# A diffusion block's head: modulation made chunk by chunk beside the first products, and sums of squares on TensorE

## The chip, the cores and the metric

One core of one Trainium2 chip. The metric is the device time in microseconds of one execution; the median of three runs is given. The compute engines are TensorE (PE; its weight loads are PEld), VectorE (DVE), ScalarE (ACT) and GpSimd (POOL); SyncE (SP) issues nearly all loads.

## What is computed

Two transformer-like blocks one after the other on 512 latent tokens (and 256 context tokens in the first part) of 1024 features, in fp32. The change touches the first norm and what feeds the first product:

```
m_l = split(silu(c) @ ada_w + ada_b, 9)        # for the latent tokens; m_c alike with c_ctx
x   = x   + 0.5 * m_l[2] * swiglu(modulate(rms_norm(x,   norm1_w), m_l[0], m_l[1]), w1, w3, w2)
ctx = ctx + 0.5 * m_c[2] * swiglu(modulate(rms_norm(ctx, norm1_w), m_c[0], m_c[1]), w1, w3, w2)
rms_norm(x, w)       = x * rsqrt(mean(x * x) + eps) * w
modulate(h, shift, scale) = h * (1 + scale) + shift
```

## The kernel before

Activations lie with the feature on the partition: 1024 features are eight chunks (KC = 8) of 128, the 768 tokens (TOK) the columns. Every large product is made of three matmuls in fp32r, whi with h_hi, whi with h_lo and wlo with h_hi. Weights come as panels of 128 x 1024 into a ring of four (raw); ScalarE rounds them to whi (round_panel, L707), GpSimd makes wlo = raw - whi (low_part, L654).

The head is all that comes before the first product. SP issues, in this order (L563 to L580): x_lat (2 MB), x_ctx (1 MB), eight small loads (vec, cond_s, lsig, lr_raw, two gate_sb, ident, rope_decay), six of the eight blocks of the modulation weights (ada_f, 1 MB each; a block holds 128 input features, the contraction index, for all 2048 columns of shift and scale), two panels, the other two blocks, two panels, and cond_b. ScalarE waits for vec and for the six transfers of small_loaded, makes the start of the log-sigmoids, Silu of the condition (cond_w), and squares x chunk by chunk (square, L724). VectorE makes the log-sigmoids (24 operations, L1807 to L1819) and adds the squares up (add_squares, L1465). TensorE does the first half of the modulation matmuls (first_modulation, L2405: four column groups of the array, 512 columns each, accumulated over the blocks into PSUM bank 5), waits for the sums and multiplies them with a column of 1/1024 (norm, L2387), spreads the factors over the partitions (L2377), does the second half of the modulation and, when ScalarE has copied the row out (L796), transposes it (L2411). VectorE adds the bias and 1 (L2248, L1456), and then, for each chunk in turn, scales x (prod, L1538); ScalarE makes h_hi (L807) and h32 (L811); VectorE makes h_lo (L1552).

The first pair of panels (first_pair, L2330) follows chunk by chunk: 12 matmuls of 384 columns for each, as soon as h_lo of the chunk is there (h_ready). Behind it stand the third panel (rounded_first, L2424) and the rest of the first layer (L2316). On VectorE the norm is followed by first_layer: differences of token halves (token_differences, L1614 to L1617), the modulation products of later parts, one chunk of 128 outputs at a time over a ring of three loads (ada_chunk, L1440), and the gated products (L1628). The first down product (first_down, L2482) needs gates from the first eight such chunks before the PSUM banks of its first panels come free (L1605).

Of the kernel before, what the change touches and what calls it, by code (L numbers as in the profile page):

```python
# [18 lines left out]
P = 128  # L19
# [16 lines left out]
ADA_COLS = ADA_PE * P  # L36
ADA_TILES = ADA_COLS // 512
# [20 lines left out]
for _s in STAGES:  # L58
# [20 lines left out]
                  gla_gate_b_b=2, conv_b_2=4, conv_w_2=16, rg_a_b_2=8, rg_x_b_2=8, rg_lambda_2=8)  # L79
# [4 lines left out]
N_VEC = _n  # L84

# [42 lines left out]
def build(nc, x_t, ctx_t, cond, ada_t, vecs, panels, lr_w, gate_w, decays, rope_grid, u_tab, level_masks, diag2, ident_h,  # L128
          ada_p, cond_t, mem_t, positions, rope_pp_h, window_bias, rg_w, out):
# [4 lines left out]
    with ExitStack() as stack:  # L134
# [34 lines left out]
        ada_f = [at(f"ada_f{kc}", ADA_COLS, R_H + 8 * kc * KB if kc < 6 else R_G + (24 + 8 * (kc - 6)) * KB) for kc in range(KC)]  # L169
        ada_row = at("ada_row", 512, R_G + 6 * KB)  # L170
        ada_w = at("ada_w", ADA_RING * D, R_ADA)
        cond_b = at("cond_b", 2 * D, R_ADA + 12 * KB)
        cond_s = at("cond_s", 2 * KC, R_TMP + 10 * KB)
        cond_w = at("cond_w", 32 * KC, R_TMP + 10 * KB + 128)
        ada_prod = at("ada_prod", D, R_ADA + 20 * KB, bf16)
        vec = at("vec", N_VEC, R_VEC)
        mods = at("mods", 2 * NMOD * KC, R_VEC + 800)
        scales = at("scales", 5 * KC, R_VEC + 1408)
        gates = at("gates", 4 * KC, R_VEC + 1664)
        eps_zero = at("eps_zero", 2, R_VEC + 1792)  # L180
        eps_t, zero_t = eps_zero[:, 0:1], eps_zero[:, 1:2]
# [7 lines left out]
        ident = at("ident", P, R_VEC + 5440)  # L189
# [51 lines left out]
        lsig = at("lsig", 16, R_VEC + 1568)  # L241
        nlsig_both = at("nlsig_both", 8, R_VEC + 1632)
        nlsig, lsig_ctx = nlsig_both[:, 0:4], nlsig_both[:, 4:8]
        ls_tmp = at("ls_tmp", 4 * 16, R_TMP + 11 * KB + 512)
# [19 lines left out]
        rope_decay = at("rope_decay", 6, R_VEC + 1376)  # L264
# [33 lines left out]
        x_loaded, vec_loaded, cond_loaded, consts = sem("x_loaded"), sem("vec_loaded"), sem("cond_loaded"), sem("consts")  # L298
# [142 lines left out]
        squares = [prod[:, 0:TOK], act_a[:, TOK:2 * TOK]]  # L441

# [119 lines left out]
        def _(sp):  # L562
            sp.dma_start(x_lat[:, :], x_t).then_inc(x_loaded, 16)  # L563
            sp.dma_start(x_ctx[:, :], ctx_t).then_inc(x_loaded, 16)
            sp.dma_start(vec[:, :], vecs).then_inc(vec_loaded, 16)
            sp.dma_start(cond_s[:, :], cond_t).then_inc(condt_loaded, 16)
            sp.dma_start(lsig[:, 0:8], decays.partition_broadcast(P)).then_inc(small_loaded, 16)
            sp.dma_start(lr_raw[:, :], lr_w).then_inc(small_loaded, 16)
            for d in range(2):
                sp.dma_start(gate_sb[d][:, :], gate_w[:, d * 256:(d + 1) * 256]).then_inc(small_loaded, 16)  # L570
            sp.dma_start(ident[:, :], ident_h).then_inc(small_loaded, 16)
            sp.dma_start(rope_pp[:, :], rope_pp_h).then_inc(small_loaded, 16)
            for kc in range(KC):
                if kc == KC - 2:
                    for s in range(2):
                        sp.dma_start(raw[:, s * PANEL:(s + 1) * PANEL], panels[s]).then_inc(raw_ready[s], 16)
                sp.dma_start(ada_f[kc][:, :], ada_p[kc]).then_inc(ada_loaded[kc], 16)
# [23 lines left out]
            first_panel(L1_DOWN[0] + 3)  # L601
            late = []
# [89 lines left out]
        def _(act):  # L692
# [21 lines left out]
            def square(m, kc):  # L714

                if m.n == 0:
                    act.wait_ge(x_loaded, 32)
                else:
                    act.wait_ge(down_evac, x_final(m.n) + kc + 1)
                if kc >= 3:  # L720
                    act.wait_ge(sum_done, m.n * (KC - 1) + kc - 2)
                buf = act_a[:, 0:TOK] if kc == 0 else squares[kc % 2]
# [59 lines left out]
            def split_gates():  # L782
                act.wait_ge(small_loaded, 96)
# [4 lines left out]
            def norm(m):  # L788
                act.wait_ge(stats_ready, m.n + 1)
                means = apart_means() if m.apart else bank(4, m.T // P)  # L790
                act.activation(rms[:, 0:m.T // P], means, ACT.Sqrt, bias=eps_t).then_inc(root_ready, 1)
                if m.n == 0:
                    round_panel(0, 1)
                    round_panel(1, 1)
                    act.wait_ge(ada_rows_done, 1)
                    act.activation(ada_row[:, :], bank(5), ACT.Copy).then_inc(ada_copied, 1)  # L796
                if m.last:
                    return
                for kc in range(KC):
# [9 lines left out]
                    if m.n == 0:  # L809
                        for j, (_, n, c0, _) in enumerate(m.segs()):  # L810
                            ins = act.activation(h32[kc][:, c0:c0 + n], prod[:, b + c0:b + c0 + n], ACT.Identity, bias=m.B[j](kc))  # L811
                        ins.then_inc(h32_done, 1)
                    if m.n == 0 and kc in (3, 4):
                        round_panel(kc - 1, 1)
# [548 lines left out]
            def cross_queries():  # L1363
# [8 lines left out]
            act.wait_ge(small_loaded, 96)  # L1372
            link(act.activation(lsig[:, 8:16], vcol("rg_lambda_2", 0, 8), ACT.Copy))
            link(act.activation(ls_tmp[:, 0:16], lsig[:, :], ACT.Abs))
            act.activation(ls_tmp[:, 0:16], ls_tmp[:, 0:16], ACT.Exp, scale=-1.0).then_inc(ls_exp, 1)
            act.wait_ge(condt_loaded, 16)
# [51 lines left out]
        def _(dve):  # L1428
# [98 lines left out]
            def norm(m):  # L1527
                if m.n:
# [1713 lines left out]
```

## Time and profile before

| What | Value |
|---|---|
| Time, median of 3 runs | 2044.85 us (2044.04 to 2046.57) |
| Profiled execution | 2042.27 us, span 2040.4 us |
| Mean granted clock of TensorE | 0.977 |
| TensorE busy | 1949.3 us (96%) |
| VectorE busy | 1024.0 us (50%) |
| ScalarE busy | 834.4 us (41%) |
| GpSimd busy | 833.7 us (41%) |
| Chain that ended last | TensorE 62%, issue 18%, VectorE 9%, GpSimd 7%, ScalarE 3% |
| First product of the first panels | 45.16 us after the span's start |

A busy share is an average over the whole span. The chain that ended last follows, from the last instruction backwards, what released each step; idle time of an engine that is not on it costs nothing. The clock column of a stretch is the granted TensorE clock as a share of 2.4 GHz.

### The profile page before, as it was taken

The page shows a single profiled execution, that of the slowest core. Times are in us where ns is not written, and L with a number is a line of the kernel's source. Part 1 is how long each engine was busy: PE and PEld are TensorE (multiplying, and loading weights), DVE is VectorE, ACT ScalarE, POOL GpSimd, SP SyncE. Part 2 cuts the span into 40 slices and gives each one's busy share as a digit, 9 for nine tenths or more (in the row PEclk, how much of TensorE's full clock was granted, in tenths as well). Part 3 has the DMA queues.
Part 4 walks back from the last instruction along what each step waited for, and adds up shares of the span by engine and source line. Part 5 has one row for each costly group of instructions (what it writes and reads, how often), then busy time and mean ns, then how long its engine had stood idle before and what let it go on. Part 6 is the DMA issues. An engine that isn't in the chain of part 4 may idle for free.

```text
span 2040.4 us, 25938 instructions
## 1 busy us (share of the span) xinstructions
PE 1949.3 (96%) x9514; PEld 1643.4 (81%) x9514; DVE 1024.0 (50%) x1527; ACT 834.4 (41%) x1276; POOL 833.7 (41%) x414
## 2 busy tenths in 40 slices
PE   4999999999989999889999999999899989999998
PEld 2999999999978875557888888877667767888886
DVE  4879877657457215964213112577964462122124
ACT  4425242434355135562532323447565453232231
POOL 1337574656424221442453443534512324353532
PEclk8999999999989999789999999999999999999999
DMA  8133343433312110002232232232211112232321
GB/s 352 53 134 141 131 163 109 160 135 115 113 62 73 72 71 31 11 21 88 83 113 93 87 108 93 103 124 83 93 52 52 65 60 93 90 107 83 113 83 62
DMA packets 53487, 197.68 MB, mean 97 GB/s; under 512 B 6320, under 2 KB 7056, under 8 KB 51600
## 3 DMA queue, kind: packets, MB, share of 16 engines
q1 hardware_dynamic: 52240, 191.47, 26.1%
q10 hardware_dynamic: 1152, 4.92, 0.7%
q8 instruction: 63, 1.03, 0.2%
q14 instruction: 32, 0.26, 0.0%
HBM read 194.27 MB, written 2.10 MB: 96 GB/s over the span
## 4 chain that ended last, share of the span: by engine, by line
PE 62%; issue 18%; DVE 9%; POOL 7%; ACT 3%; DMA 1%; SPq 0%; POOLq 0%; DVEq 0%; ACTq 0%
PE ps L2316 26%; PE ps L2445 13%; PE ps L2482 8%; POOL wlo L654 6%; PE ps L2330 2%; PE ps L2303 1%; PE ps L2304 1%; PE ps L2305 1%; PE ps L2847 1%; PE ps L2671 1%; PE ps L2662 1%; PE ps L2865 1%; DVE ada_prod L1440 1%; DVE act_a L1465 1%; DVE rg_t L2216 1%
## 5 line engine op out<-in xcount | busy, mean ns | idle before, releaser
L654 POOL TENSOR_TENSOR wlo<-raw,whi 128x1024 fp32r<-128x1024 f32 x244 | 600.0, 2469 | 985.0 <-ACT whi L707 961.6
L707 ACT ACTIVATE whi<-raw 128x1024 fp32r<-128x1024 f32 x244 | 253.6, 1053 | 271.1 <-PE ps L2316 188.4
L2316 PE MATMUL ps<-h_hi,whi 128*128 128x512 f32 (+1 forms) x960 | 352.9, 382 | 2.9 <-DVE act_a L1597 1.7
L2316 PE MATMUL ps<-h_hi,wlo 128*128 128x512 f32 (+1 forms) x960 | 350.6, 380 | 0.0
L2316 PE MATMUL ps<-h_lo,whi 128*128 128x512 f32 (+1 forms) x960 | 350.0, 379 | 0.0
L661 POOL TENSOR_TENSOR wlo<-raw,whi 128x512 fp32r<-128x512 f32 x108 | 160.3, 1499 | 133.5 <-ACT whi L875 133.1
L2316 PEld LDWEIGHTS ps<-h_hi,whi 128*128 128x128 f32 x960 | 176.6, 188 | 40.6 <-issue 5.8
L2316 PEld LDWEIGHTS ps<-h_lo,whi 128*128 128x128 f32 x960 | 176.2, 188 | 33.5 <-issue 1.0
L2316 PEld LDWEIGHTS ps<-h_hi,wlo 128*128 128x128 f32 x960 | 176.3, 188 | 32.7
L2316 PE MATMUL ps<-g_hi,whi 128*128 128x512 f32 x432 | 168.0, 389 | 0.0
L2316 PE MATMUL ps<-g_lo,whi 128*128 128x512 f32 x432 | 168.0, 389 | 0.0
L2316 PE MATMUL ps<-g_hi,wlo 128*128 128x512 f32 x432 | 168.0, 389 | 0.0
L1440 DVE SCALAR_TENSOR_TENSOR ada_prod<-ada_w,cond_b 128x1024 bf16<-128x1024 f32 x80 | 130.2, 1628 | 1.6
L875 ACT ACTIVATE whi<-raw 128x512 fp32r<-128x512 f32 x108 | 66.7, 627 | 150.2 <-PE ps L2482 113.4
L1605 DVE SCALAR_TENSOR_TENSOR x_lat<-ps,gates,x_lat 128x384 f32<-128x384 f32 (+2 forms) x120 | 59.7, 530 | 115.3 <-PE ps L2316 72.2
L1595 DVE TENSOR_TENSOR prod<-act_a,ps 128x512 f32<-128x512 f32 x22 | 15.1, 688 | 170.3 <-PE ps L2316 165.0
L2445 PE MATMUL ps<-h_hi,whi 128*128 128x384 f32 x288 | 96.3, 334 | 0.0
L2445 PE MATMUL ps<-h_lo,whi 128*128 128x384 f32 x288 | 96.3, 334 | 0.0
L2445 PE MATMUL ps<-h_hi,wlo 128*128 128x384 f32 x288 | 96.2, 334 | 0.0
L2316 PEld LDWEIGHTS ps<-g_lo,whi 128*128 128x128 f32 x432 | 81.1, 188 | 16.9
L2316 PEld LDWEIGHTS ps<-g_hi,whi 128*128 128x128 f32 x432 | 81.1, 188 | 16.9
L2316 PEld LDWEIGHTS ps<-g_hi,wlo 128*128 128x128 f32 x432 | 81.1, 188 | 16.8
(483 smaller groups left out, 3744.3 us busy)
## 6 DMA issues: line engine op xcount, KB each, us to landing
raw<-panels SPq DMA_DIRECT2D x280, 512.0 KB, 3.2
ada_w<-ada_t SPq DMA_DIRECT2D x56, 512.0 KB, 3.7
ada_f<-ada_p SPq DMA_DIRECT2D x8, 1024.0 KB, 17.0
x_lat<-x_t SPq DMA_DIRECT2D x1, 2048.0 KB, 8.0
out<-x_lat SPq DMA_DIRECT2D x8, 256.0 KB, 2.2
x_ctx<-ctx_t SPq DMA_DIRECT2D x1, 1024.0 KB, 10.0
cond_b<-cond SPq DMA_DIRECT2D x1, 1024.0 KB, 21.9
x_ctx<-mem_t ACTq DMA_DIRECT2D x1, 1024.0 KB, 4.7
```

The lines of the kernel that those rows point to most:

```text
L654: pool.tensor_tensor(wlo[:, sl], raw[:, sl], whi[:, sl].bitcast(f32), ALU.subtract).then_inc(lo_done, 1)
L661: ins = pool.tensor_tensor(half_slot(wlo, j), operand(m, j), half_slot(whi, j).bitcast(f32), ALU.subtract)
L707: act.activation(whi[:, sl], raw[:, sl], ACT.Copy).then_inc(hi_done, 1)
L875: ins = act.activation(half_slot(whi, j), operand(m, j), ACT.Copy)
L1440: dve.scalar_tensor_tensor(out=ada_prod[:, :], in0=w, scalar=1.0, in1=cond_b[:, r * D:(r + 1) * D], op0=ALU.mult, op1=ALU.mult, accum_out= ...
L1465: dve.tensor_tensor(act_a[:, 0:m.T], act_a[:, 0:m.T], squares[kc % 2][:, 0:m.T], ALU.add).then_inc(sum_done, 1)
L1605: return dve.scalar_tensor_tensor(dst, src, gate, dst, ALU.mult, ALU.add)
L2216: dve.scalar_tensor_tensor(rg_t[:, :], rg_h[:, :], 1.0, rg_t[:, :], ALU.add, ALU.mult).then_inc(rg_v, 1)
L2316: ins = pe.matmul(bank(banks + b, n), wt[:, w], a[:, at_(kc, c0):at_(kc, c0) + n], start=kc == 0 and j == 0, stop=kc == n_k - 1 and j == 2)
L2330: ins = pe.matmul(bank(banks[c] + b, n), wt[:, w], a[:, at_(kc, c0):at_(kc, c0) + n], start=kc == 0 and j == 0, stop=kc == KC - 1 and j == 2)
L2445: ins = pe.matmul(out, wt[:, w], a, start=j in (0, 1) and kc == 0 and e == 0, stop=kc == 3 and e == 2, skip_group_check=True)
L2482: ins = pe.matmul(bank(2 * ((2 * d + e) % RING) + b, cols), wt[:, w], a[:, kc * TOK + c0:kc * TOK + c0 + cols], start=kc == 0 and j == 0, ...
```

## The change

The modulation weights ada_f are laid out by output chunk: block k holds, for all 1024 input features, the 128 shift and 128 scale columns of feature chunk k. TensorE makes a row of 256 columns for a chunk from one block (modulation_rows: eight matmuls of 256 columns in four column groups, each group with two of the eight contraction parts), ScalarE copies it (modulation_row, two buffers), and two matmuls with row_sel, a matrix of two columns that adds the four groups and picks latent or context, put shift and scale on the partitions (modulation_columns). VectorE adds the bias and makes the scale of the chunk (modulation). In TensorE's order the columns of chunk kc + 2 and the rows of kc + 3 stand before the products of chunk kc.

The squares are no longer added by VectorE. For each chunk TensorE multiplies the squares of six token tiles with the column of 1/1024 and accumulates in six PSUM banks (first_sums); ScalarE has four buffers for squares. The root is made in two operations. The sums of the first four chunks, the modulation rows of chunk 0, and the other four sums follow each other.

One transfer, early, of 352 columns, stands ahead of x and holds vec, the decays, the identity and the condition. x_lat and x_ctx come in halves with a semaphore for each. lr_raw, the two gate_sb and rope_decay are issued after the first down panels. ScalarE makes Silu first and loads the table of the root ahead of the squares. The first two panels stand behind the first block of ada_f. The rounding of panel 0 stands ahead of the root, and those of panels 2 and 3 move from chunks 3 and 4 to 5 and 6.

```diff
+            sp.dma_start(early[:, :], early_h).then_inc(vec_loaded, 16)
+            for e in range(2):
+                h = slice(e * KC // 2 * LAT, (e + 1) * KC // 2 * LAT)
+                sp.dma_start(x_lat[:, h], x_t[:, h]).then_inc(x_loaded[e], 16)
+                h = slice(e * KC // 2 * CTX, (e + 1) * KC // 2 * CTX)
+                sp.dma_start(x_ctx[:, h], ctx_t[:, h]).then_inc(x_loaded[e], 16)
+            for k in range(KC):
+                sp.dma_start(ada_f[k][:, :], ada_p[k]).then_inc(ada_loaded[k], 16)
+                if k == 0:
+                    for s in range(2):
+                        sp.dma_start(raw[:, s * PANEL:(s + 1) * PANEL], panels[s]).then_inc(raw_ready[s], 16)
...
                 if m.n == 0:
-                    round_panel(0, 1)
+                    act.activation(rms[:, 0:4], ps[:, 0:4 * 512].rearrange("p (t n) -> p t n", n=512)[:, :, 0], ACT.Sqrt, bias=eps_t)
+                    act.activation(rms[:, 4:TILES], ps[:, 6 * 512:8 * 512].rearrange("p (t n) -> p t n", n=512)[:, :, 0], ACT.Sqrt, bias=eps_t)\
+                        .then_inc(root_ready, 1)
+                    modulation_row(0)
                     round_panel(1, 1)
-                    act.wait_ge(ada_rows_done, 1)
-                    act.activation(ada_row[:, :], bank(5), ACT.Copy).then_inc(ada_copied, 1)
+                    modulation_row(1)
...
+            def modulation_row(k):
+
+                act.wait_ge(ada_rows_done, k + 1)
+                act.activation(ada_row[k % 2][:, :], bank(4, ADA_COLS, k % 2 * ADA_COLS), ACT.Copy).then_inc(ada_copied, 1)
...
             act.wait_ge(vec_loaded, 16)
-            act.wait_ge(small_loaded, 96)
...
+            link(act.activation(ls_tmp[:, 0:16], lsig[:, :], ACT.Abs))
+            act.activation(ls_tmp[:, 0:16], ls_tmp[:, 0:16], ACT.Exp, scale=-1.0).then_inc(ls_exp, 1)
+            act.preload_act_table_set("sqrt_and_others")
             for kc in range(KC):
                 square(norms[0], kc)
+            round_panel(0, 1)
             norm(norms[0])
...
+            def modulation(k):
+
+                both = mods[:, :].rearrange("p (r m) -> p r m", r=2)
+                bias = vcol("ada_b", 0, 2 * KC)[:, k:k + KC + 1:KC].rearrange("p (o q) -> p o q", o=1).broadcast_to([P, 2, 2])
+                dve.wait_ge(ada_mods, k + 1)
+                dve.tensor_tensor(both[:, :, k:k + KC + 1:KC], bank(5, 4, 4 * k).rearrange("p (q r) -> p r q", r=2), bias, ALU.add)\
+                    .then_inc(mods_ready, 1)
+                dve.wait_ge(mods_ready, k + 1)
+                link(dve.scalar_tensor_tensor(scales[:, 0:2 * KC].rearrange("p (j c) -> p j c", j=2)[:, :, k], both[:, :, KC + k], 1.0,
+                                              vcol("norm1_w", k).broadcast_to([P, 2]), ALU.add, ALU.mult))
...
-            for kc in range(1, KC):
-                add_squares(norms[0], kc)
...
+            def modulation_rows(k):
+
+                pe.wait_ge(ada_loaded[k], 16)
+                for kc in range(KC):
+                    j = kc % 4
+                    ins = pe.matmul(ps[32 * j:32 * j + 32, 4 * 512 + k % 2 * ADA_COLS:4 * 512 + (k % 2 + 1) * ADA_COLS], cond_w[:, kc * 32:(kc + 1) * 32],
+                                    ada_f[k][:, kc * ADA_COLS:(kc + 1) * ADA_COLS], start=kc < 4, stop=kc >= 4)
+                ins.then_inc(ada_rows_done, 1)
+
+            def modulation_columns(k):
+
+                pe.wait_ge(ada_copied, k + 1)
+                if k:
+                    pe.wait_ge(mods_ready, k)
+                for q in range(2):
+                    ins = pe.matmul(bank(5, 2, 4 * k + 2 * q), ada_row[k % 2][:, q * P:(q + 1) * P], row_sel, start=True, stop=True)
+                ins.then_inc(ada_mods, 1)
+
+            def first_sums(kc):
+
+                pe.wait_ge(sq_ready, kc + 1)
+                for t in range(TILES):
+                    ins = pe.matmul(bank(t if t < 4 else t + 2, 1), first_squares[kc % 4][:, t * P:(t + 1) * P], ones_k[:, 0:1],
+                                    start=kc == 0, stop=kc == KC - 1)
+                ins.then_inc(stats_ready if kc == KC - 1 else sum_done, 1)
+
+            def head():
+
+                pe.wait_ge(consts, 4)
+                for kc in range(KC // 2):
+                    first_sums(kc)
+                pe.wait_ge(condt_ready, 1)
+                modulation_rows(0)
+                for kc in range(KC // 2, KC):
+                    first_sums(kc)
+                norm_spread(norms[0])
+                pe.wait_ge(sel_ready, 1)
+                modulation_columns(0)
+                modulation_rows(1)
+                modulation_columns(1)
+                modulation_rows(2)
+                for kc in range(KC):
+                    if kc + 2 < KC:
+                        modulation_columns(kc + 2)
+                    if kc and kc + 3 < KC:
+                        modulation_rows(kc + 3)
+                    for c in range(2):
...
+                    if kc == 0:
+                        modulation_rows(3)
```

## Rows read from the trace of the kernel before

**Rows 1.** Timeline of ScalarE, 15 to 20 us: start, duration, engine, line, operation [idle before].
```profile
15.45 1.28 ACT L1373 ACT_TABLE_LOAD   x1 [15.45 <-DMA rope_decay<-rope_pp_h]
16.74 0.21 ACT L1373 ACTIVATE lsig<-vec 128x8 f32<-128x8 f32 x1
...
18.88 0.61 ACT L724 ACTIVATE act_a<-x_lat 128x512 f32<-128x512 f32 x1
...
19.71 0.61 ACT L724 ACTIVATE act_a<-x_lat 128x512 f32<-128x512 f32 x1
```

**Rows 2.** Chain that ended last, 28 to 40 us: start, duration, what.
```profile
28.79 0.97 DVE act_a L1465
29.90 2.57 PE ps L2387 x12
32.49 0.28 ACT rms L791
...
33.04 1.54 PE ps L2377 x6
34.58 4.77 PE ps L2405 x32
39.37 0.61 ACT ada_row L796
```

**Rows 3.** Timeline of TensorE, first and last products of the first pair.
```profile
45.16 0.98 PE L2330 MATMUL ps<-h_hi,whi 128*128 128x384 f32 x2 [4.48 <-DVE h_lo L1552]
...
46.58 0.84 PE L2330 MATMUL ps<-h_hi,wlo 128*128 128x384 f32 x2
...
63.67 0.51 PE L2330 MATMUL ps<-h_lo,whi 128*128 128x384 f32 x2
64.01 0.51 PE L2330 MATMUL ps<-h_hi,wlo 128*128 128x384 f32 x2
```

**Rows 4.** Stretches: length, busy PE, PEld, DVE, ACT, POOL, granted clock, DMA, GB/s.
```profile
30.05:33.46 3.41, 2.83 (x14) 2.74 (x15) 0.19 (x1) 0.97 (x2) 0.00 (x0) 0.50 1.04 428
33.46:36.88 3.42, 3.42 (x18) 1.31 (x20) 0.00 (x0) 1.19 (x2) 3.10 (x2) 0.50 0.99 411
...
47.10:50.53 3.43, 3.43 (x12) 3.43 (x12) 3.36 (x7) 3.43 (x8) 0.00 (x0) 0.50 0.16 60
...
852.60:856.00 3.40, 2.81 (x24) 2.22 (x22) 3.40 (x10) 1.24 (x3) 2.77 (x3) 0.50 0.00 0
...
883.40:886.80 3.40, 3.40 (x32) 3.22 (x32) 2.49 (x7) 2.98 (x5) 2.63 (x3) 0.50 0.00 0
```

**Rows 5.** Chain that ended last, behind the norm, 61 to 151 us.
```profile
61.19 0.57 DVE t L1614
...
133.93 16.91 PE ps L2482 x96
```

**Rows 6.** Timeline of TensorE at the first down product's third panel.
```profile
133.93 0.59 PE L2482 MATMUL ps<-g_hi,whi 128*128 128x384 f32 x2 [2.84 <-DVE x_ctx L1605]
```

**Rows 7.** The page's DMA issues: count, size of each, us from issue to landing.
```profile
x_lat<-x_t SPq DMA_DIRECT2D x1, 2048.0 KB, 8.0
out<-x_lat SPq DMA_DIRECT2D x8, 256.0 KB, 2.2
```

**Rows 8.** Stretch of the loads, 5 to 10 us, columns as in rows 4.
```profile
5.00:10.00 5.00, 0.00 (x0) 0.00 (x0) 0.00 (x0) 0.00 (x0) 0.00 (x0) 1.00 0.98 413
```

**Rows 9.** Timeline of SP's queue around the first down panels.
```profile
121.35 2.93 SPq L585 DMA_DIRECT2D ada_w<-ada_t  x2
```

**Rows 10.** Timeline of TensorE, one-column matmuls at full clock.
```profile
881.36 1.05 PE L2753 MATMUL ps<-ones_k,o_sq 128*128 128x1 f32 x8
```

**Rows 11.** Timeline of VectorE in the first norm: h_lo, scaling, h_lo.
```profile
43.86 1.15 DVE L1552 SCALAR_TENSOR_TENSOR h_lo<-prod,mods,h_hi 128x512 fp32r<-128x512 f32 x2
45.05 0.75 DVE L1538 SCALAR_TENSOR_TENSOR prod<-x_lat,scales,ps 128x512 f32<-128x512 f32 x1
...
46.10 1.14 DVE L1552 SCALAR_TENSOR_TENSOR h_lo<-prod,mods,h_hi 128x512 fp32r<-128x512 f32 x2
```

More of the change, by code:

```diff
@@ L35 @@
 ADA_PE = 16
[L36 to L37 removed]
+ADA_COLS = 2 * P
 ADA_BOTH = 40
@@ L441, in build @@
         squares = [prod[:, 0:TOK], act_a[:, TOK:2 * TOK]]
+        first_squares = [a[:, b * TOK:(b + 1) * TOK] for a in (act_a, prod) for b in range(2)]
         def ada_rows(k):
@@ L601, in _ @@
             first_panel(L1_DOWN[0] + 3)
+            sp.dma_start(lr_raw[:, :], lr_w).then_inc(small_loaded, 16)
+            for d in range(2):
+                sp.dma_start(gate_sb[d][:, :], gate_w[:, d * 256:(d + 1) * 256]).then_inc(small_loaded, 16)
+            sp.dma_start(rope_pp[:, :], rope_pp_h).then_inc(small_loaded, 16)
             late = []
@@ L1527, in norm @@
             def norm(m):
-                if m.n:
-                    token_factors(m)
+                token_factors(m)
+                if m.n == 0:
+                    modulation(0)
                 dve.wait_ge(rstd_ready, m.spreads + 1)
@@ L1533, in norm @@
                         b = (kc % 2) * TOK
+                        if m.n == 0 and kc:
+                            modulation(kc)
                         if m.n == 0 and kc >= 2:
@@ L2397, in norm @@
                 ins.then_inc(rstd_ready, 1)
-            def first_modulation(k0, k1):
-                pe.wait_ge(condt_ready, 1)
-                for kc in range(k0, k1):
-                    pe.wait_ge(ada_loaded[kc], 16)
-                    for j in range(ADA_TILES):
-                        ins = pe.matmul(ps[32 * j:32 * j + 32, 5 * 512:6 * 512], cond_w[:, kc * 32:(kc + 1) * 32],
-                                        ada_f[kc][:, j * 512:(j + 1) * 512], start=kc == 0, stop=kc == KC - 1)
-                if k1 == KC:
-                    ins.then_inc(ada_rows_done, 1)
-                    pe.wait_ge(ada_copied, 1)
-                    for q in range(4):
-                        ins = pe.transpose(bank(4, P, q * P), ada_row[:, q * P:(q + 1) * P], ident[:, :])
-                    ins.then_inc(ada_mods, 1)
+            def norm(m):
+                norm_means(m)
+                norm_spread(m)
@@ new lines, in first_sums @@
+            def first_sums(kc):
[8 more added lines that the diff above has]
+                    first_sums(kc)
+                pe.wait_ge(condt_ready, 1)
+                modulation_rows(0)
[8 more added lines that the diff above has]
+                for kc in range(KC):
+                    if kc + 2 < KC:
+                        modulation_columns(kc + 2)
[3 more added lines that the diff above has]
+                        if kc == 0:
+                            pe.wait_ge(lo_done, c + 1)
+                        pe.wait_ge(h_ready, kc + 1)
+                        w = slice(c * PANEL + kc * P, c * PANEL + (kc + 1) * P)
+                        for j, (wt, a) in enumerate(((whi, h_hi), (whi, h_lo), (wlo, h_hi))):
+                            for b, c0, n in halves(TOK):
+                                ins = pe.matmul(bank(2 * c + b, n), wt[:, w], a[:, hidden_at(kc, c0):hidden_at(kc, c0) + n],
+                                                start=kc == 0 and j == 0, stop=kc == KC - 1 and j == 2)
+                        if kc == KC - 1:
+                            ins.then_inc(panel_done, 1)
+                    if kc == 0:
+                        modulation_rows(3)
@@ L3025, in _ @@
             pe.sem_inc(panel_done, RING)
-            first_modulation(0, KC // 2)
-            norm(norms[0])
-            first_modulation(KC // 2, KC)
+            head()
             first_layer()
@@ L3221 @@
         "ada_t": np.ascontiguousarray(a["ada_w"][0].T.reshape(NMOD * KC, P, D)),
-        "vecs": vecs,
+        "early_h": early,
         "panels": panels,
```

101 lines of the change are left out of this document (41 added, 60 removed).

## The prediction, made before the changed kernel ran

> **What bounds the kernel now.** I read the page first (TensorE is busy for 96% of the span, so that little outside the head and the joints can be won), then the chain of waits of the first 46 us, then TensorE's timeline and the granted clock around the first product, then the chain behind it. The chain is to be read as one string of single steps: until 15.4 us everything waits for the last of eight small loads, because ScalarE waits for seven of them before its first operation [rows 1]; then come log-sigmoids and seven additions on VectorE, the six mean matmuls from 29.90, the root, the spreading, modulation matmuls in 32 records, a copy at 39.37 and four transposes [rows 2]; the first product stands at 45.16 after 4.48 us of idle TensorE [rows 3]. TensorE does nothing useful in these 45 us, and it enters the products at half clock: the granted clock is 0.50 in the stretch that ends at 50.53, a pair of products takes 0.84 us there and 0.51 at full clock, where pairs follow each other every 0.34 [rows 3, 4].
>
> Where the head's end is worth something has to be read behind it. From 61.19 the chain runs over VectorE's token differences and modulation products, loads and ScalarE, and holds no TensorE piece until 133.93, where TensorE stood idle for 2.84 us [rows 5, 6]. So what sets the end is when **VectorE leaves the first norm** (61.19 now); the products of the first pair, whose last two start at 64.01 [rows 3], have 2.84 us to spare.
>
> **Loads.** Eight small loads leave the front, and one of 180 KB leads. The row of a lone store of 256 KB lands in 2.2 us [rows 7]; issued at 0.75, the new one should land at about 3.3. The x arrays now come in halves. The queue moves 413 GB/s [rows 8], and x_lat's 2.1 MB landed 8.0 us after issue [rows 7]: the first half (1.75 MB with what leads it) is then there at about 7.9. The last modulation chunk has 12.8 MB in all at or before it and lands at about 2.5 + 31 + 1.2 = 34.7, long before its matmuls (53, below). Loading by chunk costs nothing here and binds nothing. The four small loads that go behind the first down panels are issued by SP in the time before the load at 121.35, for which SP waits on VectorE [rows 9]; the panels of that stage are issued before them. I cost them at nothing; uncovered they would be four issues of about 0.5.
>
> **ScalarE's start.** From 3.3: a table load of 1.28 and Silu, a second for Exp, a third for the roots, and three activations of 0.2: 3.3 + 3.84 + 0.8 = 7.9, as late as the data. The load at 15.45 took 1.28 and its activation began at 16.74, at once [rows 1]. The Trainium skill (ScalarE: Activation LUTs, section What ACT_TABLE_LOAD costs) adds a drain of 1.38 us to each; by it the squares would begin 2 to 4 us later and all below with them. The trace contradicts it for an engine that has little in flight. Then a square of 512 and 256 columns takes about 0.83 to 1.0 (18.88 to 19.71 [rows 1]); the first sum can begin at 9.0.
>
> **Sums on TensorE.** Seven additions on VectorE of 0.97 each [rows 2] and the log-sigmoids ahead of them leave the path. In comes, for each of eight chunks, what before was done once: six fp32 matmuls of one column, 12 records, 2.57 us at half clock [rows 2]. They are bound by weight loads, so splitting them does not make them cheaper. ScalarE makes squares every 0.83, so TensorE is the bound from the first sum on. 8 x 2.57 = 20.6, and chunk 0's modulation matmuls (half of the columns, twice the number: 4.77 / 4 = 1.2 mixed, 0.9 taken) stand between the halves: 9.0 + 20.6 + 0.9 = **30.5**, against 32.46 now. The price hangs on the clock. What the rows show of one-column matmuls: two groups of eight records ran from 881.36 on, 1.05 each (one is shown [rows 10]), and the clock was 0.50 from 883.4; the stretch at 852.6, with TensorE busy for 2.81 of 3.4 us in 128-column matmuls, stayed at 0.50; and the sums of the head themselves filled most of a stretch at 0.50, while the clock came back only behind the modulation matmuls, at 36.88 [rows 4]. So I take half clock for all of them. At full clock a group of 12 costs about 12 x 0.13 = 1.6 (1.05 for 8 [rows 10]).
>
> **From the sums to the first product.** Two roots instead of one of 0.28: 0.5; the reciprocal with its handovers 0.25 (32.77 to 33.04); spreading 1.5 [rows 2]; the two-column matmuls of chunk 0, four records of 2.57 / 12: 0.85; VectorE's two small operations 0.4 (a ScalarE operation of that size takes 0.21 [rows 1]): 34.0. First scaled chunk 1.05, to 35.1. VectorE's next instruction is no longer the second chunk's but chunk 1's modulation: TensorE's rows of chunk 1 0.9, the copy 0.4 (0.61 for 512 columns [rows 2]), columns 0.85, until 35.8, and 0.4: 36.3. Then the second chunk 1.05 and h_lo of the first 1.2 (45.05 to 46.10 and 43.86 to 45.05 [rows 11]), with handovers: **38.7**, 6.4 before now. The 4.77 of modulation matmuls, the copy of 0.61 and the transposes are gone from this stretch; two chunks of the same work, 3.9 with copies, have come in.
>
> **In the pair.** Now it lasts from 45.16 to 64.5. It is eight chunks of 12 products (2.08 at full clock, 3.9 at half). The change puts rows of five chunks and columns of five into TensorE's own order between them: 5 x (0.43 + 0.45) = 4.4 at full clock, in a place where TensorE is busy. A chunk thus costs 3.0 at full and 5.6 at half clock; VectorE's turn goes from 2.24 (43.86 to 46.10 [rows 11]) to 2.7, and ScalarE gets a copy of 0.4 in each. Half clock lasted 5.4 us from the first product on [rows 3, 4]; I take the same, until 44.1. Followed step by step: products of chunk 0 38.7 to 42.9, rows of 3 to 43.8, copy, columns of 3 at about 44.8. VectorE has scaled chunk 2 by 40 and now waits 3 us for these columns. From there it follows TensorE by turns of 3.0: columns of 4 at 47.8, of 5 at 50.7, of 6 at 53.7, of 7 at 56.7; two more turns, each 2.7 with ScalarE's rounding of two panels in the way, end h_lo of the last chunk at **62.0**, and the products at 64.0. So 6.4 us won ahead of the first product are spent again: 4.4 for work moved among products, the rest in waits, and VectorE leaves the norm 0.8 later than the 61.19 of now [rows 5].
>
> **Sum.** The profiled execution took 2042.27 (span 2040.4), 2.6 under the median of 2044.85. 2042.3 + 0.8 = 2043.1; against the median **2045.7**. Unknown terms: the start of the sums 8.4 to 9.7 (-0.5 to +0.5); the clock back between 3.8 us after matmuls of full width begin (33.04 to 36.88, spreading and modulation [rows 2, 4]) and 8 us: -0.7 to +1.5; VectorE beside GpSimd's low part of panel 1, 0 to +0.4. Together 2044.1 to 2047.7, and the three runs spread by 2.5.
>
> **The rivals.** A, the sums warm the clock. TensorE has then no gap for 21 us, which speaks for it. After two or three groups at half clock the rest cost 1.6: the sums end at about 23.5, the first product is at 31, the products run at full clock at once, and VectorE leaves the norm at about 52: -9.5 us, 2035.5. Against it stand the stretches at 883 and 30 [rows 4, 10]. The Trainium skill (TensorE: Matmul & The Clock Gate, section Why this matters for your kernels) says to keep TensorE busy continuously for the full clock; by that rule this is the case that comes. 13%.
> B, the interleaved work is nearly free (weight loads slip under products, ScalarE's copies come early): the pair then takes 20.5 instead of 25.3 and the gain in front stays: -4, 2041. Against it: the columns need a copy that waits for rows in TensorE's own order. 4%.
> C, slower: the clock comes back late. In the pair TensorE now alternates products with two-column matmuls and waits for copies, and each chunk at half clock costs 5.6 instead of 3.0. Each us of half clock more costs 0.5; from about 51 on, 12 us after the first product, it is over +4.1 (VectorE at 65.3, 2049.0), and if it never comes back in the pair +12, 2057. For it: the 0.50 stretch at 852.6 with busy 128-column work [rows 4]; against it: 384-column products took the clock up in 5.4 us. 5%.
> D, the change doesn't do what it says ahead of time: the chunks are ready two to three ahead only in program order. That is my forecast's own mechanism, and its time is in it.
>
> **How the numbers follow.** Forecast 78%, A 13%, B 4%, C 5%. About 0.2% (4.1 us) is what a measurement of this kernel can tell from no change. Faster: A and half of B, 15%. Slower: C, 5%. Same 80%. The range takes the forecast's 2044.1 to 2047.7 with the spread of the runs, and B: 2041.0 to 2048.7.
>
> **What would show it.** The mean matmuls in eight groups of about 2.6 us from 9 to 30.5, granted clock not full there; first product at 38.7; VectorE's first token difference at 62; TensorE's idle before the third down panel grown from 2.8 to about 4. Sums of 1.6 us, or a first product before 34, make me wrong on A's side; a clock still half at 51 on C's.

## The result, and the profile after the change

The changed kernel takes 2052.0 us (median of eight runs, 2050.7 to 2054.9), the kernel before 2044.8 in the runs beside it: a ratio of 1.0039 (95% interval 1.0030 to 1.0047), 7.2 us slower. The forecast was 2045.7, with 2041.0 to 2048.7 as its range; it was wrong, on the side to which it gave one chance in twenty. The profiled execution after took 2052.48 us, span 2050.7, with a mean granted clock of 0.981.

TensorE's time in the first 70 us, grouped by form: line, operation, tiles and count | busy, mean ns of one.

```profile
L2426 PE MATMUL ps<-ada_f,cond_w 128*32 128x256 f32 x128 | 11.2, 481 | 0.0
L2443 PE MATMUL ps<-ones_k,act_a 128*128 128x1 f32 x48 | 10.5, 352 | 9.0 <-ACT act_a L730 9.0
L2443 PE MATMUL ps<-ones_k,prod 128*128 128x1 f32 x48 | 10.5, 352 | 0.0
L2436 PE MATMUL ps<-eps_zero,ada_row 128*128 128x2 f32 x32 | 5.5, 276 | 1.5 <-ACT ada_row L830 1.5
```

The sums take 21.0 us and the two-column matmuls 5.5, near what the forecast gave them. The modulation rows (L2426) take 11.2; the forecast had given them some 5. TensorE's timeline (start, duration, engine, line, operation, tiles, records, in brackets the idle time before and what ended it) shows where:

```profile
8.99 5.25 PE L2443 MATMUL ps<-ones_k,act_a 128*128 128x1 f32 x24 [8.99 <-ACT act_a L730]
14.11 5.26 PE L2443 MATMUL ps<-ones_k,prod 128*128 128x1 f32 x24
19.30 1.93 PE L2426 MATMUL ps<-ada_f,cond_w 128*32 128x256 f32 x16
21.16 5.28 PE L2443 MATMUL ps<-ones_k,act_a 128*128 128x1 f32 x24
26.30 5.26 PE L2443 MATMUL ps<-ones_k,prod 128*128 128x1 f32 x24
...
34.41 1.93 PE L2426 MATMUL ps<-ada_f,cond_w 128*32 128x256 f32 x16
36.85 1.01 PE L2436 MATMUL ps<-eps_zero,ada_row 128*128 128x2 f32 x4 [0.50 <-ACT ada_row L830]
37.79 1.93 PE L2426 MATMUL ps<-ada_f,cond_w 128*32 128x256 f32 x16
...
41.10 0.99 PE L2474 MATMUL ps<-h_hi,whi 128*128 128x384 f32 x2
...
45.22 1.17 PE L2426 MATMUL ps<-ada_f,cond_w 128*32 128x256 f32 x16
...
47.44 1.07 PE L2426 MATMUL ps<-ada_f,cond_w 128*32 128x256 f32 x16
48.44 0.62 PE L2474 MATMUL ps<-h_hi,whi 128*128 128x384 f32 x2
```

A chunk's rows take 1.93 us at half clock (1.2 GHz; the clock is read here from the length of the matmuls, 0.84 or 0.51 for a pair of products) and 1.07 at full clock. They answer to the 32 records of [rows 2]. The clock column of a stretch can't be used for this: all through the first 50 us it stands at 1.00, also where the sums take the 2.6 us a group of half clock (columns as in [rows 4]):

```profile
20.00:25.00 5.00, 5.00 (x30) 4.04 (x23) 0.00 (x0) 1.34 (x3) 2.34 (x1) 1.00 1.01 423
```

So the forecast's sign "granted clock not full there" holds by the lengths alone. The first product stands at 41.10, 4.1 before the 45.16 of [rows 3]. From 48.44 on a chunk of the pair takes 3.65 us (2.08 of products, 1.07 of rows, 0.5 of columns), and VectorE follows:

```profile
47.62 0.17 DVE L1579 TENSOR_TENSOR mods<-ps,early 128x4 f32<-128x4 f32 x1 [3.67 <-PE ps L2436]
...
58.53 0.17 DVE L1579 TENSOR_TENSOR mods<-ps,early 128x4 f32<-128x4 f32 x1 [1.05 <-PE ps L2436]
...
67.09 0.56 DVE L1643 TENSOR_TENSOR t<-h 128x384 f32<-128x384 f32 x1
```

It waits 3.67 us for the columns of chunk 3 and 0.6 to 1.5 us in each later turn, and leaves the norm at 67.09, where it was 61.19 [rows 5]: 5.9 later. The chain that ended last, further on:

```profile
123.56 3.43 DVE ada_prod L1455 x2
...
129.62 2.21 DVE ada_prod L1455 x2
...
140.93 18.47 PE ps L2549 x96
159.40 48.04 PE ps L2512 x276
```

The third down panel begins at 140.93, 7.0 after the 133.93 of [rows 5], and takes 18.47 instead of 16.91; the piece of 48.04 begins 8.6 later than before (159.40 and 150.84). So 5.9 of the loss is made in the head and 1.1 on the way to the third panel. The other 1.6 is clock: TensorE idles 4.88 us ahead of the third panel instead of 2.84 [rows 6], and afterwards runs at half clock:

```profile
141.00:144.40 3.40, 3.40 (x11) 3.40 (x12) 2.73 (x7) 1.15 (x2) 2.28 (x2) 0.51 0.00 0
```

(the stretch, with the columns of [rows 4]). The kernel before kept 1.00 in the same place.

These 8.6 us still stand at 872.56, where a piece of 10.50 us begins that began at 864.01 before. The profiled spans differ by 10.3. The rest comes later and does not follow the head: from that piece to a pause near 1620 us this execution took 748.3 us and that of e5 748.4; the kernel before and eight of the others took 744.5 to 746.1. So a single time of this kernel says little to 2 us, and where only one run was made its place at the piece of 10.50 us is given as well.

### The profile page after: what moved, and what is told of

Same layout as the page of the kernel before. It is cut to its first block, busy times and chain, and to the rows that moved or that the text cites. A ratio compares the mean times of both kernels' runs of the same rounds, so it can differ in the third digit from the quotient of the medians.

```text
span 2050.7 us, 26307 instructions
## 1 busy us (share of the span) xinstructions
PE 1973.1 (96%) x9690; PEld 1668.6 (81%) x9690; DVE 1020.5 (50%) x1533; ACT 836.3 (41%) x1283; POOL 836.0 (41%) x414
## 4 chain that ended last, share of the span: by engine, by line
PE 82%; DVE 10%; issue 3%; ACT 3%; DMA 1%; POOL 0%; SPq 0%; DVEq 0%; ACTq 0%
PE ps L2335 44%; PE ps L2512 13%; PE ps L2549 8%; PE ps L2349 2%; PE ps L2322 1%; PE ps L2324 1%; PE ps L2323 1%; PE ps L2913 1%; PE ps L2737 1%; PE ps L2728 1%; PE ps L2809 1%; PE ps L2443 1%; DVE ada_prod L1455 1%; PE ps L2931 1%; DVE rg_t L2245 1%
## 5 line engine op out<-in xcount | busy, mean ns | idle before, releaser
L2549 PE MATMUL ps<-g_hi,whi 128*128 128x384 f32 x352 | 90.2, 337 | 5.8 <-DVE x_ctx L1634 4.9
```

What stands on the lines that cost most here:

```text
L2549: ins = pe.matmul(bank(2 * ((2 * d + e) % RING) + b, cols), wt[:, w], a[:, kc * TOK + c0:kc * TOK + c0 + cols], start=kc == 0 and j == 0, ...
```

## The experiments

An "exit" below is the start of VectorE's first token difference, where it leaves the first norm: 61.19 before, 67.09 after.

**VectorE adds the squares again.** On the changed kernel. ScalarE's squares go back to their old buffers with it, and the root is one operation again (not shown).

```diff
+            for kc in range(1, KC):
+                add_squares(norms[0], kc)
...
-                for kc in range(KC // 2):
-                    first_sums(kc)
                 pe.wait_ge(condt_ready, 1)
                 modulation_rows(0)
-                for kc in range(KC // 2, KC):
-                    first_sums(kc)
+                pe.wait_ge(sum_done, KC - 1)
+                for t in range(TILES):
+                    ins = pe.matmul(bank(5, 1, 64 + t), act_a[:, t * P:(t + 1) * P], ones_k[:, 0:1], start=True, stop=True)
```

> One part undone: VectorE adds the squares up again and TensorE multiplies once (six one-column matmuls); all else is the changed kernel's. Theory (the eight groups of one-column matmuls, 20.7 us at half clock, stand on the path): the groups' time leaves, squares and additions end at about 16.5, the one group at 19.1 instead of 31.6, the first product at about 28.6 instead of 41.1, VectorE leaves the first norm at about 54.6, and the time falls by 12.5 us against the changed kernel, to about 2039.5, 5 under the kernel before. Rival (what binds the head is the arrival of the modulation blocks or TensorE's row matmuls, and the sums lie beside them): the first product comes after 35 and the time falls by less than 6 us.

2039.53 us, ratio 0.9976 (0.9966 to 0.9985). The seven additions run beside squares that are due anyway, and the sums are one group:

```profile
16.17 0.96 DVE L1476 TENSOR_TENSOR act_a<-act_a 128x768 f32<-128x768 f32 x1
```

```profile
17.18 2.72 PE L2452 MATMUL ps<-ones_k,act_a 128*128 128x1 f32 x12 [0.77 <-DVE act_a L1476]
```

The first fence is the last addition in VectorE's timeline, the second TensorE's. Exit 56.06, 11.0 before that of the changed kernel, and 12.5 us less time (11.6 at the piece of 10.50 us). The first product comes 11.8 earlier, at 29.29, in place of the 28.6 expected, and the exit is 1.5 later than expected. So this part of the change costs 11 to 12.5 and all the rest together is worth 5.7: with the sums on VectorE this head is faster than the kernel before.

**Small loads later.** The four transfers behind the first down panels are issued after the panels of the next stages.

```diff
-            sp.dma_start(lr_raw[:, :], lr_w).then_inc(small_loaded, 16)
...
                     if k not in late:
                         ada_load(k)
+                if st == STAGES[L1_SIZES[0] + 3]:
+                    sp.dma_start(lr_raw[:, :], lr_w).then_inc(small_loaded, 16)
...
```

> The changed kernel with its four small loads (lr_raw, two gate_sb, rope_decay) issued 20 us later, where SP waits for VectorE. Theory (between VectorE's leaving the norm, +5.9, and the third down panel, +7.0, 1.1 us were lost because these loads delay the landing of two panels, so that GpSimd's low parts run beside VectorE's modulation products, and the longer idle of TensorE let its clock fall for 1.6 us): 1 to 2.5 us less than the changed kernel. Rival (the small loads are hidden by SP's wait): no change, within 0.7 us.

2050.68 us, ratio 1.0029 (1.0018 to 1.0041). The median is 1.4 under the changed kernel's, but the intervals overlap, and nothing moved in the profile: exit 67.23, third panel at 141.22, and TensorE's wait there is still 5.04.

```profile
141.22 0.98 PE L2550 MATMUL ps<-g_hi,whi 128*128 128x384 f32 x2 [5.04 <-DVE x_ctx L1635]
```

The small loads aren't what lengthens that wait, and GpSimd's low parts stand in one row as in the changed kernel (114.14 to 126.18). Whether they cost anything elsewhere stays open.

**Rows of half width.** Rows and copies of 128 columns for chunks 2 to 7. This leaves out the scale of these chunks, so that the kernel no longer computes what the reference does.

```diff
+                    n = ADA_COLS if k < 2 else P
...
-                                    ada_f[k][:, kc * ADA_COLS:(kc + 1) * ADA_COLS], start=kc < 4, stop=kc >= 4)
+                                    ada_f[k][:, kc * ADA_COLS:kc * ADA_COLS + n], start=kc < 4, stop=kc >= 4)
```

> The changed kernel with the modulation rows of chunks 2 to 7 at half width: the 128 scale columns are neither multiplied nor copied, so shift and scale of these chunks are not the reference's. Theory F (a floor for each record of a matmul with 32 weight columns, whatever its moving width): the 16 records of a chunk still take 1.9 us at half and 1.0 at full clock. Theory C (cost by moving columns): they take half of that, 1.0 and 0.5, and a chunk of the pair takes 3.1 us instead of 3.6.

```profile
44.44 1.08 PE L2429 MATMUL ps<-ada_f,cond_w 128*32 128x128 f32 x16
...
51.42 0.64 PE L2429 MATMUL ps<-ada_f,cond_w 128*32 128x128 f32 x16
```

With half the columns TensorE's rows take 1.08 instead of 1.93 at half clock and 0.64 instead of 1.07 at full: the price goes by columns, with some 0.2 that stays. Theory F, a floor for each record, falls. The one run took 2049.74. Its exit is at 66.06, only 1.0 earlier, and the piece of 10.50 us 0.4 earlier; in this execution the clock came back at about 36.4, was lost again before the first product at 40.33, and the products of chunk 1 still began at half clock (1.01 at 47.88), so this run doesn't price the columns in time. Once the clock is full, a chunk of the pair takes 3.22 us (51.99 to 55.22), near the 3.1 of theory C.

**Warm clock ahead of the sums.** Twelve matmuls of 512 columns, whose results nobody reads, ahead of first_sums.

```diff
+                for _ in range(12):
+                    pe.matmul(bank(4), ones_k[:, :], ones_k[:, 0:1].broadcast_to([P, 512]), start=True, stop=True)
                 for kc in range(KC // 2):
                     first_sums(kc)
```

> The changed kernel with twelve matmuls of 512 columns on a constant ahead of the first sum, in the idle time of TensorE before x lands; their result is not used. Theory N (one-column matmuls do not hold the clock): the first one or two groups of sums take about 1.4 us, the later ones 2.6 again, and the gain is 2 to 5 us. Rival A (uninterrupted one-column matmuls hold it): all eight groups take 1.4, the sums end near 22, and the time falls by about 10 us.

```profile
1.32 12.81 PE L2451 MATMUL ps<-ones_k 128*128 128x512 f32 x24 [1.32 <-POOL cond_w L654]
13.98 2.73 PE L2443 MATMUL ps<-ones_k,act_a 128*128 128x1 f32 x24
16.57 2.82 PE L2443 MATMUL ps<-ones_k,prod 128*128 128x1 f32 x24
19.32 1.86 PE L2426 MATMUL ps<-ada_f,cond_w 128*32 128x256 f32 x16
21.11 5.28 PE L2443 MATMUL ps<-ones_k,act_a 128*128 128x1 f32 x24
```

TensorE's timeline: the first 48 sum records take 5.4 us, half of the 10.4 in the changed kernel, and then the clock is gone, though TensorE had no pause. Two stretches, with the columns of [rows 4]:

```profile
5.00:19.00 14.00, 14.00 (x67) 8.90 (x65) 4.15 (x24) 7.42 (x15) 0.00 (x0) 1.00 1.01 409
20.00:45.00 25.00, 23.27 (x122) 19.32 (x114) 7.51 (x17) 6.91 (x15) 4.70 (x2) 0.50 1.00 411
```

A long run of one-column matmuls neither takes the clock up (the changed kernel) nor keeps it (here). Rival A falls. Nothing was won in time: the twelve matmuls last until 14, so the sums begin 5.0 us later than the 8.99 of the changed kernel, which uses up what the faster groups give. The first product stands at 41.05 (41.10), the exit at 67.70, later than the 67.09, and the piece of 10.50 us at 872.39 (872.56). The 2050.07 of the one run, 2.0 under the median, is therefore not a gain made in the head.

**All rows and columns ahead of the pair.** On e1; ScalarE's copies and VectorE's modulation move with them.

```diff
-                modulation_columns(0)
-                modulation_rows(1)
...
+                for k in range(KC):
+                    if k >= 2:
+                        modulation_columns(k - 1)
+                    if k:
+                        modulation_rows(k)
...
```

> e1_vector_sums, with all modulation rows and columns of the eight chunks ahead of the first product, on TensorE, ScalarE and VectorE alike. Theory I (the interleaving of modulation with products is worth something, although each chunk of the pair takes 3.65 us of TensorE with it): the seven chunks after the first become a chain of 1.93 (rows at half clock), 0.5, 1.0 (columns), 3.4 each from 22.6 us on, or 2.1 each where the clock is full; the first product stands at 44 to 50 instead of 29.3, the pair then runs at VectorE's own turn of 2.24, VectorE leaves the norm at 60 to 66 instead of 56.1, and the time is 2043.5 to 2049.5. Theory J (TensorE's 3.65 us turns cost as much as the chain would): within 1 us of 2039.5.

2052.55 us in one run, 13.0 over e1 and 3 beyond the upper end of theory I. The seven chunks take 3.38 us each, all at half clock; here that of chunk 3:

```profile
29.62 1.93 PE L2422 MATMUL ps<-ada_f,cond_w 128*32 128x256 f32 x16
32.05 1.01 PE L2432 MATMUL ps<-eps_zero,ada_row 128*128 128x2 f32 x4 [0.50 <-ACT ada_row L825]
```

First product at 50.71, exit 66.83 (e1: 56.06), the piece of 10.50 us at 872.43 (861.01). In these two executions the interleaving is worth 10.8 us at the exit, although each chunk of the pair costs 1.57 more with it. Part of that is clock: rows with columns and waits didn't bring it up in 23 us, and at full clock the expectation had 2.1 a chunk. Of the 13.0 only 11.4 are there at 872 us; the rest is the slow later stretch named above.

**Rows and columns one chunk earlier.** On e1.

```diff
                 modulation_rows(2)
+                modulation_columns(2)
+                modulation_rows(3)
                 for kc in range(KC):
...
+                        if c == 0 and kc + 3 < KC:
+                            modulation_columns(kc + 3)
+                    if kc + 4 < KC:
+                        modulation_rows(kc + 4)
```

> e1_vector_sums, with the rows of chunk 3 ahead of the first product, the columns of chunk kc+3 between the two panels' products of chunk kc, and the rows of chunk kc+4 behind them. Theory (TensorE's own order sets VectorE's pace): the 4.43 us for which VectorE waits for the columns of chunk 3 shrink to about 1.5, since they no longer stand behind all products of chunk 0 at half clock, but the last columns stand behind half a chunk of products less and no more: VectorE leaves the norm 0.5 to 1 us before 56.1, 2038.5 to 2039.1. Rival (the wait of 4.43 is itself what makes the norm long): 3 us less, 2036.5.

2039.66 us, ratio 0.9980 (0.9970 to 0.9989): no different from e1's 2039.53, and less than the 0.5 to 1 expected. The profiled execution is the fastest of ten (2037.56; the slowest took 2044.75), with the exit at 52.99. But by the lengths of its matmuls the clock was up from about 24.4 to 27.8 and again from 31.2 on, in e1 from 35.9 on, so that its 3.1 us are not the edit's alone. VectorE's wait for the columns of chunk 3, 4.43 in e1, is gone in e6, where it waits for no later columns longer than 1.14. What that gave by itself can't be told from this pair.

**Warm rows, and both together.** The twelve unread matmuls on e1, in TensorE's idle time ahead of the first rows; then on e6.

```diff
                 pe.wait_ge(condt_ready, 1)
+                for _ in range(12):
+                    pe.matmul(bank(4), ones_k[:, :], ones_k[:, 0:1].broadcast_to([P, 512]), start=True, stop=True)
                 modulation_rows(0)
```

> e1_vector_sums, with twelve matmuls of 512 columns whose results nobody reads, in TensorE's idle time ahead of the first modulation rows (1.3 to 14.1 us). Theory (what remained of the head's price is the half clock, and rows of 256 columns with sums of only 12 records keep a clock that is full): rows 1.07 instead of 1.93, sums 1.6 instead of 2.7, first product at about 26 instead of 29.3, and the second chunk of products at about 30 instead of 37.4; VectorE leaves the norm at about 49, 2032 to 2034. Rival (as in e4, the clock is gone when it is needed): rows of chunk 1 on at 1.93, 2038.5 to 2040.

> The edits of e6_one_chunk_earlier and e7_warm_rows together on e1_vector_sums. If both theories hold: 0.5 to 1 us under e7, 2031.5 to 2033.5. If the clock is lost: as e6, 2038.5 to 2039.1.

2037.92 (ratio 0.9973, 0.9960 to 0.9985) and 2037.56 (0.9961, 0.9947 to 0.9975): between theory and rival, and close to the rival, 0.6 and 0.9 under its lower ends. In the first the sums take 1.50 and rows 1 and 2 take 1.07, but at 26.27 TensorE has waited 1.71 us for a copy, and the products begin at half clock:

```profile
26.27 0.61 PE L2434 MATMUL ps<-eps_zero,ada_row 128*128 128x2 f32 x4 [1.71 <-ACT ada_row L826]
27.45 0.98 PE L2474 MATMUL ps<-h_hi,whi 128*128 128x384 f32 x2 [0.57 <-DVE h_lo L1566]
```

In the second the clock is gone earlier, in the rows of chunk 1, behind the sums and waits of 0.45 and 0.58 us:

```profile
20.55 1.81 PE L2424 MATMUL ps<-ada_f,cond_w 128*32 128x256 f32 x16
```

The exits are 54.18 and 52.57. The matmuls started late, at 3.6, behind ScalarE's Silu, and pushed the first rows from 14.5 to 17.2 and 15.8.

**Rows of a quarter width.** On the changed kernel, 64 columns for chunks 2 to 7. The edit is that of e3 with 64 for P; it leaves out three quarters of the shift and scale of these chunks.

> The changed kernel, with modulation rows of 64 instead of 256 columns for chunks 2 to 7, and copies alike; it leaves out three quarters of their shift and scale. Theory R (the step that failed is the price of the rows, which goes by columns): by the rows of e3_half_rows and the changed kernel (0.2 us and 0.43 for each 128 columns at full clock, 0.85 at half) these rows cost 0.43 at full and 0.64 at half clock, the first of which is what the prediction took. The first product stands at 39.8 instead of 41.1, a chunk of the pair takes 3.0 instead of 3.65, VectorE leaves the norm at 62 (67.1 minus 2 x 1.3 and 4 x 0.64), where the prediction had it, and the time is 2046 to 2048. Rival S (something else in the pair holds VectorE back, such as the columns, the copies or the clock): it leaves at 65 or later, 2050 or more.

```profile
46.15 0.43 PE L2429 MATMUL ps<-ada_f,cond_w 128*32 128x64 f32 x16
46.51 0.62 PE L2477 MATMUL ps<-h_hi,whi 128*128 128x384 f32 x2
...
49.49 0.62 PE L2477 MATMUL ps<-h_hi,whi 128*128 128x384 f32 x2
```

2048.69 us, ratio 1.0021 (1.0012 to 1.0031). These rows cost what the forecast had taken for real ones at full clock (0.43), and a chunk of the pair takes the forecast's 3.0. Exit 63.07 (theory R 62, rival S 65 or later); 3.4 us less than the changed kernel against the 4 to 6 expected. Theory R holds at the exit, for 4.0 of the 5.1 by which the forecast missed it (the first product stands at 40.63, not 39.8). In time it holds for 3.4 of the 6.3 by which the forecast missed: the third panel, at 137.50, lies 74.4 behind the exit, where it was 72.7 behind it before, and takes 18.29.

**TensorE's waits filled.** On e6: eleven unread matmuls ahead of the wait for Silu, and one each behind rows 0, behind the sums, and behind rows 1 and 2.

```diff
+                for k in (1, 2):
+                    modulation_rows(k)
+                    pe.matmul(bank(0), ones_k[:, :], ones_k[:, 0:1].broadcast_to([P, 512]), start=True, stop=True)
+                    modulation_columns(k)
```

> e6_one_chunk_earlier, with matmuls of 512 columns whose results nobody reads: eleven from 1.3 us on, ahead of the first rows, and one each behind rows 0, behind the sums, and behind rows 1 and 2, in the places where TensorE waits 0.5 to 0.8 us. Theory (the clock fell in e7 and e8 at 26.8 and 20.7 us, behind waits and sums; with the waits filled it stays full): rows of chunks 1 to 3 at 1.07, first product at about 26, VectorE leaves the norm at 49 to 51, 2034.5 to 2036.5. Rival (the sums and two-column matmuls themselves let the clock fall): rows at 1.93 again and the fillers on the path on top, 2038 to 2040.

```profile
17.27 1.50 PE L2456 MATMUL ps<-ones_k,act_a 128*128 128x1 f32 x12 [0.87 <-DVE act_a L1476]
18.63 1.11 PE L2459 MATMUL ps<-ones_k 128*128 128x512 f32 x2
...
23.06 1.07 PE L2424 MATMUL ps<-ada_f,cond_w 128*32 128x256 f32 x16
24.06 1.13 PE L2465 MATMUL ps<-ones_k 128*128 128x512 f32 x2
25.39 0.61 PE L2434 MATMUL ps<-eps_zero,ada_row 128*128 128x2 f32 x4 [0.20 <-ACT ada_row L826]
...
26.93 0.61 PE L2476 MATMUL ps<-h_hi,whi 128*128 128x384 f32 x2
```

2034.10 us, ratio 0.9955 (0.9939 to 0.9972), 0.4 under the range expected: 18 us under the changed kernel and 10 under the kernel before, the best of this study. Every matmul of the head after 14 us is at full clock; the exit is 49.61. The edit does two things at once: the unread matmuls ahead of the rows start at 1.32 and not at 3.6, and the waits are filled. Against e8, which has the same order and only the late warm-up, the two give 3.5 us; they weren't tried apart. The Trainium skill (TensorE: Matmul & The Clock Gate, section Why this matters for your kernels) advises against long idle gaps of TensorE between bursts of matmuls. This run agrees (0.2 to 0.9 us of gap up to the products, clock kept), but short gaps weren't enough elsewhere: e8 lost the clock behind gaps of 0.45 and 0.58 us, and e4 lost it with no gap at all.

## Why the prediction was wrong, step by step

- **Loads, ScalarE's start: right.** Squares from 7.91 (forecast 7.9), first sum 8.99 (9.0). ScalarE's three table loads took 1.28 each. The second has its activation at once behind it, as in [rows 1], and the third starts at 5.01, at once behind an activation; no drain shows. Behind the first and third ScalarE waits for data:

```profile
3.48 1.28 ACT L1392 ACT_TABLE_LOAD   x1
4.77 0.22 ACT L1392 ACTIVATE ls_tmp<-ls_tmp 128x16 f32<-128x16 f32 x1
```

- **Sums: right.** 5.2 for two groups, half clock throughout, 20.7 for eight (forecast 20.6). What the forecast did not draw from it is how dear they are beside the additions that they replace: 12.5 us in e1.
- **Rows of a chunk: wrong, and the cause of most of the late exit.** The forecast divided 4.77 us for four old blocks [rows 2] by four, 1.2 "mixed", and then took 0.9 at half and 0.43 at full clock. An average over both clocks can't lie above its half-clock value. The weight loads of the kernel before show it; a new group of four every 0.85 us at half clock and every 0.43 at full:

```profile
35.37 0.20 PEld L2405 LDWEIGHTS ps<-ada_f,cond_w 128*32 128x32 f32 x4 [0.66 <-issue]
36.22 0.20 PEld L2405 LDWEIGHTS ps<-ada_f,cond_w 128*32 128x32 f32 x4 [0.66 <-issue]
...
37.41 0.12 PEld L2405 LDWEIGHTS ps<-ada_f,cond_w 128*32 128x32 f32 x4 [0.31 <-issue]
```

  (In that view the next groups start at 37.84 and 38.27.) A chunk's rows are four such groups of half as many columns: 4 x 0.43 = 1.7 at half clock, 0.85 at full, and 0.2 of tail: 1.93 and 1.07, as measured. Three chunks short by 1.0, one by 0.3, four by 0.64 is 5.9 in all; the exit missed by 5.1. e3 shows that the price goes by columns, and e9, with rows that cost what the forecast took at full clock, brings the chunk back to 3.0 and the exit to 63.07.
- **Sums' end to first product:** 8.2 forecast, 9.6 measured (31.5 to 41.1), two chunks' rows at 1.0 more less small savings. **Clock back** some 4.3 us after the first product, 5.4 forecast. **Chunk of the pair** 3.65, not 3.0. **VectorE waits** 3.67 for the columns of chunk 3, forecast 3.
- **Norm to end: wrong as well, the second term.** The forecast put what is added behind the exit at nothing and gave no reason, though it expected TensorE's idle time there to grow. Measured: +1.1 to the third panel, +1.6 of half clock there. VectorE's six modulation products took 10.9 us (123.56 to 134.43) instead of 8.6. The first took 3.4 and the fourth 2.2, beside GpSimd's low parts, of which four stood in one row:

```profile
113.86 12.02 POOL L658 TENSOR_TENSOR wlo<-raw,whi 128x1024 fp32r<-128x1024 f32 x4 [11.25 <-ACT whi L711]
128.53 2.20 POOL L665 TENSOR_TENSOR wlo<-raw,whi 128x512 fp32r<-128x512 f32 x1 [2.65 <-ACT whi L891]
```

  Before, GpSimd had done the row by 118.1, and the first product, at 118.83, took 1.2; a later one took 2.1 beside the 1.5 us low part at 123.57. So the first product is what was added. No run was made for this overlap, but the kernels differ in it by themselves. In e6 GpSimd is done at 110.88, ahead of VectorE's first product, and that product takes 1.2:

```profile
104.83 6.05 POOL L658 TENSOR_TENSOR wlo<-raw,whi 128x1024 fp32r<-128x1024 f32 x2 [0.50 <-ACT whi L711]
```

```profile
111.62 1.23 DVE ada_prod L1451 x2
```

  (GpSimd's timeline and the chain.) In e1, e2, e3, e4, e5, e7, e8, e9 and e10 it begins beside a low part and takes 3.4. In every one of the twelve kernels each slow product ends 1.1 us behind the low part beside it (123.56 + 3.43 against 113.86 + 12.02 here), as if it ran only then; and the low part at 128.53, begun beside a running product, took 2.2, where one in e1 took 1.3. That VectorE waits there for GpSimd is read from these traces. e2 rules out the small loads as the reason for the row; why the panels arrive as they do, and why the clock falls at the third panel in the new kernels, stays open.
- **Range.** The forecast's own terms, -1.2 and +2.4 about 2045.7, give 2044.5 to 2048.1 and not 2044.1 to 2047.7; 2052.0 lies outside both, and outside 2041.0 to 2048.7.
- **Rivals.** A fell (e4, and the sums at half clock throughout in the changed kernel). B fell too: a chunk with the interleaved work takes 3.65 against 2.08. Against doing that work ahead it was still the better order (e5). C's side came, by another cause: the clock came back early enough, the rows were dear.
- **Chances.** "Slower" got 5%, for a late clock alone; no chance was kept for a wrong price, and the one that wasn't checked against its own clock decided.

## What to carry to other kernels

Before a price is taken from a row that spans a change of clock, split the row at the change, and test the split: the two prices must enclose the average. Moving a reduction from VectorE to TensorE is a bad trade where each piece is a one-column matmul with a full weight load at half clock: 20.7 us against seven hidden additions. And in this head TensorE's clock was worth more than the order of the work (the order of e6 gave nothing in time; the warm-up and the filled waits put on it in e10 gave 5.6 us): fill the waits with wide matmuls that nobody reads, start them before the first real one, and end them before it is due.

## What the hardware showed that was not expected

- Sums of one column ran at 1.35 us for twelve records after the clock had been brought up, and at 2.6 once it fell; it fell with TensorE busy for 14.00 of 14.00 us up to 19 (e4).
- Rows and two-column matmuls with 0.5 us waits, TensorE busy for 19.25 of 22.70 us, never brought the clock up (e5); the same kinds of work kept it, once it was up and the waits were filled (e10).
- The clock column of a stretch showed 1.00 from 22.8 to 45.5 in e5, where rows took 1.93, the half-clock length, and in the changed kernel from 10 to 41, where sums and rows had their half-clock lengths. In a head, the length of a known matmul is the safer reading.
- Where the clock comes back in the head differs between kernels with like heads (35.9 in e1, 31.2 for good in e6, 36.4 and lost again in e3), so exits of single profiles can't be compared to the last us there.
- VectorE's modulation product of 1024 elements took 1.2 us alone and 3.4 or 2.1 to 2.2 where it began beside a low part of GpSimd, ending 1.1 us behind it (123.56 + 3.43 and 113.86 + 12.02 in the changed kernel; e6, without the overlap at its first product, 1.2).
